# Where the fifth of eight large cache copies begins: in a decoder step's first stage, or in its third

## The reference

```
h = RMSNorm(x);  z = h @ w_in
A  sparse attention over compressed blocks, selected blocks and a window of 512
B  dilated attention, windows 128, 512 and 2048 with dilations 1, 4 and 16
C  a gating MLP inside chunks of 128
x = x + (sum of the gated branches) @ w_out
x = x + relu(RMSNorm(x) @ w_up)**2 @ w_down;  final RMSNorm
```

```
kv_ext = concatenate([buf, new_rows], axis=1)
bufs.append(kv_ext[:, -min(window, wb + s_len):])
```

## Time and profile before

| | |
|---|---|
| time, median of 3 runs | 1829.16 us (1821.88 to 1833.83) |
| the profiled execution: its own time | 1845.35 us |
| its span, first to last instruction | 1843.7 us |
| TensorE busy | 1733.6 us, 94% of the span |
| VectorE, ScalarE, GpSimd busy | 36%, 18%, 10% |
| mean granted TensorE clock | 0.959 |
| moved by DMA | 323.10 MB, of it 129.65 MB on GpSimd's queue (q0) |

### The profile page before, as it was taken

One profiled execution on the slowest core, in us unless ns is written; L12 is line 12 of the kernel. 1 busy time (PEld: TensorE's weight loads), 2 busy tenths in 40 slices (PEclk: granted clock), 3 DMA queues, 4 the chain that ended last, 5 costly groups with the idle time before them and its releaser, 6 DMA issues. The chain is left out here.

```text
span 1843.7 us, 27027 instructions
## 1 busy us (share of the span) xinstructions
PE 1733.6 (94%) x10424; PEld 1376.6 (75%) x10424; DVE 672.6 (36%) x1583; ACT 327.6 (18%) x836; POOL 184.3 (10%) x329
## 2 busy tenths in 40 slices
PE   8996899999989999999996898888998999999997
PEld 3785799999968777777773455656887888888885
DVE  3432244443321333333222202102466766543234
ACT  2210034433320222222220121210000000000000
POOL 0000100000000001000006575540000000000000
PEclk9998699999989999999996989988999999999999
DMA  9999433333339987421309999895521222222221
GB/s 315 348 353 306 133 103 104 101 100 108 115 132 330 338 306 271 138 94 47 99 33 322 314 343 322 293 328 196 178 79 48 92 69 92 84 77 91 69 92 49
DMA packets 150339, 323.10 MB, mean 175 GB/s; under 512 B 18690, under 2 KB 87619, under 8 KB 149187
## 3 DMA queue, kind: packets, MB, share of 16 engines
q1 hardware_dynamic: 118498, 178.87, 29.7%
q0 software_dynamic: 27104, 129.65, 20.3%
q10 hardware_dynamic: 4608, 12.85, 2.1%
HBM read 303.89 MB, written 109.25 MB: 224 GB/s over the span
## 5 line engine op out<-in xcount | busy, mean ns | idle before, releaser
L1435 PE MATMUL bank<-hT,wring 128*128 128x272 f32 x1408 | 346.7, 397 | 1.1 <-PEq L1216 1.1
L1435 PEld LDWEIGHTS bank<-hT,wring 128*128 128x128 f32 x1408 | 260.4, 191 | 58.5 <-issue 10.5
L956 PE MATMUL bank<-wring,w 128*128 128x128 f32 x2048 | 247.3, 278 | 1.1 <-DVE hidp L871 1.1
L956 PEld LDWEIGHTS bank<-wring,w 128*128 128x128 f32 x2048 | 237.0, 193 | 10.0 <-issue 9.5
L1868 POOL DMA_DIRECT2D ring<-in_sel_pages x256 | 140.9, 551 | 321.3 <-issue 277.7
L2253 PEld LDWEIGHTS bank<-hT,xk 128*128 128x128 f32 x512 | 104.5, 210 | 54.3 <-issue 30.4
L2253 PE MATMUL bank<-hT,xk 128*128 128x272 f32 x512 | 140.4, 432 | 0.0
L2506 PE MATMUL bank<-hT,wring 128*128 128x272 f32 x392 | 95.4, 392 | 0.0
L2506 PEld LDWEIGHTS bank<-hT,wring 128*128 128x128 f32 x392 | 74.5, 190 | 15.4
L2506 PE MATMUL bank<-aT,wring 128*128 128x272 f32 x352 | 85.9, 392 | 0.0
L319 POOL DMA_DIRECT2D out_new_dil<-in_cache_dil x24 | 15.1, 635 | 675.1 <-POOLq L1216 343.5
(11 more groups left out here) (365 smaller groups left out, 2293.8 us busy)
## 6 DMA issues: line engine op xcount, KB each, us to landing
wring<-in_w SPq DMA_DIRECT2D x147, 512.0 KB, 4.4
out_new_dil<-in_cache_dil POOLq DMA_DIRECT2D x8, 8176.0 KB, 33.6
wring<-in_cmp_pages SPq DMA_DIRECT2D x256, 128.0 KB, 2.2
ring<-in_sel_pages POOLq DMA_DIRECT2D x256, 64.0 KB, 4.5
ring<-in_sel_pages SPq DMA_DIRECT2D x256, 64.0 KB, 4.1
out_new_dil<-in_cache_dil POOLq DMA_DIRECT2D x8, 2032.0 KB, 12.8
ring<-in_dil_k SPq DMA_DIRECT2D x9, 1024.0 KB, 8.3
ring<-in_dil_k POOLq DMA_DIRECT2D x9, 1024.0 KB, 7.4
```

Of the source, the lines that this page charges most:

```text
L956: last = pe.matmul(banks[6 + c % 2][:, P * part:P * part + P].rearrange("p (g a s) -> p g a s", g=G, s=8), w1[:, kv, 8 * hf + jj, :], x[:, ...
L1435: mm = pe.matmul(banks[6 + hf][:, 0:HT], ring_slot(wr, u)[:, k * P:k * P + P], hT[:, k, HT * hf:HT * hf + HT], start=(k == 0), stop=(k == ...
```

## The change

The first call of `bulk_copies` issues four copies where it issued five. The second call issues "all that is left", so it issues 28 where it issued 27. No copy is left out or altered, and the order of the list stays.

```diff
             @block.gpsimd
             def _(pool):
 
                 pool.wait_ge(s_sgl, 16 * 9)
-                bulk_copies(pool, 5)
+                bulk_copies(pool, 4)
```

## The result

The changed kernel takes 1823.14 us (median of 20 runs, 1811.58 to 1832.77) where the kernel before, run beside it, takes 1836.05 us (median of 20, 1821.88 to 1844.77). The ratio is 0.9934, with a 95% interval of 0.9912 to 0.9955: 0.7% faster, 12.9 us between the medians. One run of before there, at 6208 us and in a slow state, is left out. The forecast gain of 16.5 us lies between the two. It would be a ratio of 0.9910, just outside the interval of the first measurement and inside that of the second. The forecast time, 1812.7 us, was missed by 10.4 us.

What follows compares the result with a forecast made beforehand. The prediction took TensorE as bound, with 19.6 us lost waiting at the first stage's end for GpSimd's copy. Meeting -16.5, clock 0, moved copy 0 took 1829.16 to 1812.7 us; range 1802 to 1824.

Steps and rivals of the forecast that it cites:

- The meeting waits for GpSimd's own copy: End of first stage, L460: GpSimd's DRAIN lasts until its fifth copy lands; without it the compressed stage starts 16.5 us earlier.
- GpSimd's next DRAIN looks bad and costs nothing: At L460 after the change: GpSimd's DRAIN lasts about 62 us but ends about 157.4, before VectorE's at 173.0.
- The moved copy costs the dilated stage nothing: Dilated stage: one more copy priced at 0, covered by weight tiles requested six ahead; copies end at 779.3 us.
- The bound of 23.9 us: Dilated stage: upper bound on the moved copy's cost, if TensorE lost the copy's whole share of the DMA engines.
- The clock at the new start is 1.2 GHz: Compressed stage's start: TensorE's clock as low as before, rising only with the chunk products; term 0, ends 8.4 gain, +2.
- the clock stays up: Rival, 8 in 100: clock full from the compressed stage's start, 8.4 us more, 24.9 us gained in all, 1804.3 us.
- The sum: Whole kernel: -16.5 + 0 + 0 = -16.5 us, from 1829.16 to 1812.7 us, 0.9% faster.
- A smaller wait in plain runs: Rival, 11 in 100: copies 5% faster unprofiled, first-stage meeting 8 us earlier, half the gain gone, about 1821 us.
- The ring runs dry: Rival, 4 in 100: weights late at L1435 early in the dilated stage, TensorE loses 23.9 us, 1836.6 us.
- The change doesn't do what it says: Rival, 5 in 100: the meeting at L460 waits for something other than GpSimd's copy; time stays at 1829 us.

Runs made afterwards that it cites:

- e1: Kernel before with six large copies issued in the first stage instead of five: 1857.04 us, ratio to before 1.0121.
- e10: Kernel before with five first-stage copies, the fifth a small one of 2032 KB, the large one moved to the dilated stage: 1823.06 us, ratio to before 0.9928.
- e8: Changed kernel with the fifth large copy issued by SyncE behind its stores at the end of the first stage: 1838.83 us, ratio to before 1.0005.
- e6: Changed kernel measured and profiled once more, no edit: 1821.09 us, ratio to before 0.9906 (0.9874 to 0.9938), 18.6 us between the medians.
- e4: Changed kernel plus five extra TensorE matmuls with constants in the 3 us gap at the first stage's end: 1817.37 us, ratio to before 0.9909.
- e11: Changed kernel plus three extra TensorE matmuls with constants at the first stage's end: 1811.62 us over six runs, ratio to before 0.9881.
- e12: Kernel e11 plus five more extra matmuls in TensorE's wait near the compressed stage's end: 1813.82 us, ratio to before 0.9869.
- e2: Kernel before with no copy issued in the first stage, all 32 in the dilated stage: 1825.07 us, ratio to before 0.9947.
- e3: Changed kernel with the fifth large copy left out altogether, for timing only: 1823.53 us, ratio to before 0.9948.
- e9: Changed kernel with the fifth large copy issued by GpSimd inside the compressed stage, behind its tiny transfers: 1830.32 us, ratio to before 0.9961.

## Why the prediction was right, and where it was not

*The meeting waits for GpSimd's own copy.* Right, and shown from four sides: without the copy the meeting is at 172.9 (after), with a second one at 215.1 (e1), with a small one at 173.3 (e10), and with the same large copy open on SyncE's queue at 174.0 (e8). The forecast of 16.5 us for this step met 16.7.

*GpSimd's next DRAIN looks bad and costs nothing.* Right: 62.8 us long, over at 155.9.

*The moved copy costs the dilated stage nothing.* Right: 424.1 to 424.7 us with none, one and five copies more, and 424.1 with the fifth left out. The bound of 23.9 us was far too careful. The copies ended at 760.3, not 779.3: the stage began 10 us earlier than forecast, the two pairs took 126.5 us instead of 130, and the rest 118 instead of 123.

*The clock at the new start is 1.2 GHz, since "up to there nothing in the program differs".* This is the step that failed as an argument. The fall before 172 us was one execution's: of the six profiles with the same gap three kept the clock, and of the changed kernel itself one did (its first) and one did not (e6). I took a property of one execution for one of the program. The term itself, 0, holds in the average of the profiles (347.1 against 346.3 us, good to some 3 us), by luck and not for the reason that I gave: the short gap trades the middle level for the best or the worst. The 8 in 100 for "the clock stays up" were too few for any single execution, and right in that it isn't the median's story. Its price was also too low: 8.4 us counted L833 and the first chunk but left out the scores, which take 1.99 us instead of 3.78; the compressed stage shows 10.2. The page of the Trainium skill, "TensorE: Matmul & The Clock Gate", section "Why this matters for your kernels", advises against long gaps between bursts of matmuls, as idleness takes the clock down. At 3.05 us the clock held in three of six profiles here; at 0.3 us it held at the restart in all three (e4, e11, e12), though in e4 it fell around a later wait of 1.13 us.

*The sum.* 16.5 us forecast; 12.9 and 18.6 us measured between medians. The forecast time of 1812.7 us against 1823.14 is another matter. Of the 10.4 us, 6.9 are the starting point, a median of three runs (1829.16) where twenty gave 1836.05, and the rest is the smaller gain. That the time still lies below the upper end of the range, 1824, by under 1 us, is luck.

In plain runs the gain is mostly smaller than the 16.7 us of the meeting. The meeting is at 172.6 to 173.3 us, and no copy lies beside the page loads, in the changed kernel, e6, e10, e2 and e3; their ratios are 0.9934, 0.9906, 0.9928, 0.9947 and 0.9948, on average 12.4 us. The forecast's 0.9910 lies outside the intervals of the changed kernel's first measurement, of e2 and of e3. Why is open, and the clock is one candidate. While e2 and e3 were timed, the runs of before spent 119.6 us on average at the lower clock (twice the missing clock times the span), some 17 of them in the wait, where they cost nothing; e2 spent 121.2 and e3 115.6. By that estimate these two worked 13 to 19 us longer at the lower clock, and at 0.4 to 0.6 us for each (the slopes of the batches) it would cost them 5 to 11 us. Beside e6 it was 127.5 against 110.7 us, equal without the wait, and there the gain is the full one. So the clock's term is likely a loss in some measurements and not always 0.

The profiled pair's 30.9 us are 16.7 for the meeting, 10.2 for the two extremes of the clock that happened to be profiled, and 4 in later stages, of which the gathers' 2.1 lie well inside their own scatter (281.8 and 291.6 us in the two profiles of before). A fairer pair is before and e6, whose clocks both fell and rose late: 23.8 us, of which 16.6 are the meeting, 0.2 the compressed stage and 6.4 the gathers.

*The rivals.* "A smaller wait in plain runs": two more profiles with the fifth copy in place had the meeting at 189.9 and 190.0, and in plain runs e1's sixth copy cost 22 to 23 us where its profile had the meeting 25.5 us later. So a wait that is much shorter is unlikely; one shorter by a few us would fit the mean gain of 12.4 us and was not tested. "The ring runs dry" happened nowhere in the dilated stage, but the like of it did, with pages in place of weights, in e8 and e9, where a copy runs beside loads that nothing has preloaded. "The change doesn't do what it says" fell.

## What to carry to other kernels

Before a meeting of all engines, ask what each issuer still has under way: a transfer that nobody needs can hold everybody, if its issuer's DRAIN waits for it. Put such a transfer where the loads beside it are requested well ahead and the meeting is far (here the dilated stage, six tiles ahead), not where a stage begins empty. And when a short idle gap of TensorE is left, a pair of profiles says little about the clock behind it: profile each kernel twice, compare stage by stage, and try to fill the gap with matmuls that nobody reads if they fit (likely 5 us or more here, by six runs).

## What the hardware showed that I had not expected

- The DRAIN of GpSimd's queue lasted as long as its open copy (32.2, 59.4, 62.8 and, for a small copy, 12.0 us), SyncE's 0.4 us with the same 8 MB copy open.
- On SyncE's own queue, page loads of 128 KB issued behind the 8 MB copy held TensorE 20.6 us; with the copy on GpSimd's queue they landed in 8.6 us at the median (180 to 216 us), and TensorE still waited 16.5 us.
- Behind the same gap of 3.05 us the granted clock stayed full in three profiles and fell in three (once only during the scores), and where it fell it stayed at 0.50 through all of L833 (13.9 us, TensorE busy throughout). Behind longer gaps (3.9 to 44.9 us) it fell always, and rose during the scores or early in L833 in four profiles of five. With a gap of 0.3 us it was full at the restart in three of three, but fell for 3 us around a wait of 1.13 us in one of them (e4).
- Much of the spread of single runs (a standard deviation of 5 to 7 us for before and the changed kernel) goes with the mean granted clock. The start of the compressed stage (10 us between its levels) and the stage of gathers (281.8 to 295.7 us over the profiles) carry it; the MLP varied by 0.8 us.
